# Moving the convolution tables, the joins and the query norms in the second block's input projections

## The reference, cut to what matters

```python
h  = modulate(x, norm1_g[l], sh1, sc1)           # 512 tokens
hc = modulate(ctx, norm1_g[l], csh1, csc1)       # 256 context tokens
zl_hy, zl_gla, zl_gdn = split_last(h @ w_in, IN_SIZES)
...
# Hyena: short_conv over z, then twice, with gate x1 and then x2:
conv = irfft(rfft(y, n=2*l) * filt_f[:, o], n=2*l)[:, :l]
y = gate * (conv + d_skip[o] * y)
# gated delta rule: q and k of each head are divided by their norms
shared = (l2norm(to_heads(q)) * GDN_D ** -0.5, l2norm(to_heads(k)), to_heads(v))
...
x = x + g1 * y
x = x + g2 * sq_relu_mlp(modulate(x, norm2_g[l], sh2, sc2), w_mlp1[l], w_mlp2[l])
```

## Time and profile before

| | |
|---|---|
| median of three runs | 1901.78 us (1901.45 to 1909.95) |
| the profiled execution | 1891.71 us |
| its span, first to last instruction | 1889.9 us |
| PE busy, share of the span | 1772.2 us, 94% |
| DVE, ACT, POOL busy | 52%, 34%, 19% |
| mean granted PE clock | 0.974 |
| projections of the second block | to about 1196 us |
| `stage_hyena` | 1196.6 to about 1235 us |

### The profile page before, as it was taken

How to read it: one execution, slowest core, us unless ns; L and a number is a source line. 1 busy time by engine, 2 the same in 40 slices (tenths; PEclk the granted TensorE clock), 3 DMA queues, 4 the chain that set the end, 5 groups by cost and what they waited for, 6 DMA issues and landing times. The chain is left out here.

```text
span 1889.9 us, 45257 instructions
## 1 busy us (share of the span) xinstructions
PE 1772.2 (94%) x19313; PEld 1322.5 (70%) x19313; DVE 989.0 (52%) x1839; ACT 651.8 (34%) x1233; POOL 361.6 (19%) x517
## 2 busy tenths in 40 slices
PE   6999989999989979989989998889998999999998
PEld 5777667777766763343357776677777788888887
DVE  7666445555467651121177876546777674323334
ACT  5555444534423222131245623022212343213421
POOL 1000053534444331101100000013222011001100
PEclk9999989999999989989999999889999999999999
DMA  6222111101139579999971223310001423222221
GB/s 230 81 92 77 58 52 48 43 22 52 53 130 360 199 299 374 410 407 409 408 295 56 84 79 106 122 36 14 25 21 53 169 100 123 96 94 94 96 100 45
DMA packets 77216, 265.11 MB, mean 140 GB/s; under 512 B 11552, under 2 KB 13984, under 8 KB 75744
## 3 DMA queue, kind: packets, MB, share of 16 engines
q1 hardware_dynamic: 65824, 233.92, 33.6%
q10 hardware_dynamic: 5616, 15.99, 2.4%
q0 software_dynamic: 5584, 12.40, 1.8%
HBM read 248.17 MB, written 21.50 MB: 143 GB/s over the span
## 5 line engine op out<-in xcount | busy, mean ns | idle before, releaser
L224 DVE TENSOR_TENSOR weights_lo<-ring,weights_hi 128x1024 fp32r<-128x1024 f32 (+1 forms) x134 | 165.8, 1240 | 139.5 <-ACT weights_hi L220 139.5
L220 ACT CAST weights_hi<-ring 128x1024 fp32r<-128x1024 f32 (+1 forms) x134 | 137.1, 1026 | 234.3 <-PE ps L250 223.0
L249 PE MATMUL ps<-wide_b_round,weights_hi 128*128 128x512 f32 (+1 forms) x368 | 134.6, 366 | 0.0
L248 PE MATMUL ps<-mlp_hi,weights_hi 128*128 128x512 f32 (+1 forms) x327 | 121.3, 371 | 1.2 <-DVE weights_lo L224 1.1
L249 PE MATMUL ps<-mlp_lo,weights_hi 128*128 128x512 f32 (+1 forms) x327 | 120.4, 368 | 0.0
L250 PE MATMUL ps<-mlp_hi,weights_lo 128*128 128x512 f32 (+1 forms) x327 | 120.4, 368 | 0.0
L248 PE MATMUL ps<-h_tail_round,weights_hi 128*128 128x512 f32 x232 | 90.8, 391 | 0.9 <-DVE weights_lo L224 0.7
L248 PE MATMUL ps<-wide_a_round,weights_hi 128*128 128x512 f32 x216 | 91.0, 422 | 0.6 <-DVE wide_b_round L742 0.6
L4706 POOL TENSOR_TENSOR h_scaled<-h_scaled 128x512 f32<-128x512 f32 x32 | 33.8, 1055 | 296.7 <-ACT h_scaled L4680 296.7
L249 PE MATMUL ps<-h_tail_rest_round,weights_hi 128*128 128x512 f32 x232 | 90.3, 389 | 0.0
L250 PE MATMUL ps<-h_tail_round,weights_lo 128*128 128x512 f32 x232 | 90.3, 389 | 0.0
(11 more groups left out here) (714 smaller groups left out, 4175.0 us busy)
## 6 DMA issues: line engine op xcount, KB each, us to landing
ring<-stream_in SPq DMA_DIRECT2D x207, 512.0 KB, 3.6
moe_ring<-stream_in SPq DMA_DIRECT2D x112, 512.0 KB
wide_b<-stream_in SPq DMA_DIRECT2D x32, 512.0 KB
w_mod<-w_mod_in ACTq DMA_DIRECT2D x24, 512.0 KB, 6.9
hy_mod<-w_mod_in SPq DMA_DIRECT2D x8, 512.0 KB, 6.9
gates_parked<-gates_late SPq DMA_DIRECT2D x14, 256.0 KB, 2.6
na_rel<-rel_in POOLq DMA_DIRECT2D x4, 640.0 KB, 4.1
xT<-xT_in SPq DMA_DIRECT2D x4, 512.0 KB, 5.9
```

Of the source, the lines that this page charges most:

```text
L220: act.copy(self.hi[:, i % self.n, at:], w[:, at:]).then_inc(self.cast.sem, self.cast.up())
L224: ins = eng.tensor_tensor(self.lo[:, i % self.n, at:], self.unit(i)[0][:, at:], self.hi[:, i % self.n, at:], ALU.subtract)
L248: pe.matmul(out, left[0], right[0], start=start, stop=False, **kw)
L249: pe.matmul(out, left[0], right[1], start=False, stop=False, **kw)
```

## The change

- SP: the filter and `hy_fwd` are issued ahead of the small moves, and all four quarters of `hy_inv` behind them, still ahead of the moves and all in the projections. They go to the three modulation slots and to a free row of `d_gate`, so they wait for the last modulation step and for the last sum of the query norms (`summed` 8).
- The sixteen modulation steps are over by unit 19; before, two of them lay in units 20 and 21.
- All four joins are on POOL.
- The query norms of the four heads, before after (20,1), (21,0), (21,1) and behind spectrum 1, are now after (21,0), (21,1), spectrum 1 and spectrum 2. DVE's order at the end is spectra 0, head 2, spectra 1, head 3.
- `stage_hyena` has no loads of `hy_inv`, and eight slots for its eight pieces of `w_mod`, so that SP waits for none of them.

```diff
-SIDE.update({at: ("qb", i) for i, at in enumerate(((20, 1), (21, 0), (21, 1), (22, 0)))})
+SIDE.update({at: ("qb", i) for i, at in enumerate(((21, 0), (21, 1), (22, 0), (22, 1)))})
...
-MOD_AT = {12: 2, 13: 1, 14: 1, 15: 2, 16: 2, 17: 1, 18: 2, 19: 3, 20: 1, 21: 1}
+MOD_AT = {12: 2, 13: 1, 14: 1, 15: 2, 16: 3, 17: 2, 18: 3, 19: 2}
...
-        inv = mod_slot[1:3]
+        inv = [mod_slot[1], mod_slot[2], mod_slot[0], d_gate[:, 1, :]]
... tensor
                 conv.spectrum(pe, 0)
                 conv.spectrum(pe, 1)
+                side(number["qb", 2])
+                conv.spectrum(pe, 2)
                 side(number["qb", 3])
-                conv.spectrum(pe, 2)
                 conv.spectrum(pe, 3)
... vector
-                    if u == N - 2:
-                        join(0)
-                        join(1)
                 leave(N - 1)
                 conv.spectra(dve, 0, 0)
+                side(number["qb", 2])
+                conv.spectra(dve, 0, 1)
                 side(number["qb", 3])
-                conv.spectra(dve, 0, 1)
... gpsimd
-                join(2)
-                join(3)
+                for i in range(4):
+                    join(i)
... sync
-                for f in range(LongConv.EARLY):
-                    sp.wait_ge(mod_stepped.sem, mod_stepped.at(MOD_STEPS - 2 + f))
-                    sp.dma_start(inv[f], k.dram["hy_inv"][:, f, :]).then_inc(inv_in.sem, inv_in.up(16))
                 sp.wait_ge(saved.sem, saved.at(16))
                 sp.wait_ge(w.done.sem, w.done.at(place["gk", 0] + 1))
                 sp.dma_start(k.B[:, :, :], k.dram["filter"]).then_inc(filter_in.sem, filter_in.up(16))
+                sp.wait_ge(k.used, k.after(N - 1))
+                for f in range(2):
+                    sp.dma_start(k.ring[:, 4 + f, :], k.dram["hy_fwd"][:, f, :]).then_inc(filter_in.sem, filter_in.up(16))
+                sp.wait_ge(mod_stepped.sem, mod_stepped.at(MOD_STEPS))
+                sp.wait_ge(summed.sem, summed.at(8))
+                for f in range(NF):
+                    sp.dma_start(inv[f], k.dram["hy_inv"][:, f, :]).then_inc(slot_in[(f + 1) % 3].sem, slot_in[(f + 1) % 3].up(16))
                 sp.wait_ge(pads.sem, pads.at(2))
                 sp.wait_ge(left_a.sem, left_a.at(place["gk", 0] + 1))
                 sp.wait_ge(left_v.sem, left_v.at(dve_before[place["gk", 0] + 1]))
                 ... the twelve small moves
-                sp.wait_ge(k.used, k.after(N - 1))
-                for f in range(2):
-                    sp.dma_start(k.ring[:, 4 + f, :], k.dram["hy_fwd"][:, f, :]).then_inc(filter_in.sem, filter_in.up(16))
... stage_hyena
-    SLOTS_W = 6
+    SLOTS_W = 8
...
-                for f in range(conv.EARLY, NF):
-                    sp.dma_start(late_inv[:, f - conv.EARLY, :], k.dram["hy_inv"][:, f, :]).then_inc(inv_in.sem, inv_in.up(16))
                 for n in range(DB):
-                    if n >= SLOTS_W:
-                        sp.wait_ge(mod_used.sem, mod_used.at(n - SLOTS_W + 1))
                     sp.dma_start(wm[:, n % SLOTS_W, :], k.dram["w_mod"][4 * DB + n]).then_inc(...)
...
-                    if o == 0 and f >= conv.EARLY:
-                        pe.wait_ge(inv_in.sem, inv_in.at(16 * (NF - conv.EARLY)))
```

More of the change, by code:

```diff
@@ L3107, in stage_mixer_in @@
             e_done, x_done, gate_chain = k.sig("e_done"), k.sig("gate_min_done"), k.sig("gate_chain")
-            mod_in, mod_stepped = [k.sig(f"mod_landed{i}") for i in range(3)], k.sig("mod_steps")
-            folds, inv_in = k.sig("hy_halves"), k.sig("inv_landed")
+            slot_in, mod_stepped = [k.sig(f"mod_landed{i}") for i in range(3)], k.sig("mod_steps")
+            folds = k.sig("hy_halves")
             def has_dve(i):
@@ L3444, in scale_x @@
                         h_scaled.sem, h_scaled.up())
[L3446 to L3449, removed]
                 def mod_step(m):
@@ L3453, in mod_step @@
                     c, x, total = k.silu_c[:, n, 0:1], mod_slot[m % 3], mod_total[:, half * T:(half + 1) * T]
-                    dve.wait_ge(mod_in[m % 3].sem, mod_in[m % 3].at(16 * (m // 3 + 1)))
+                    dve.wait_ge(slot_in[m % 3].sem, slot_in[m % 3].at(16 * (m // 3 + 1)))
                     if n == 0:
@@ L3539, in load_mod @@
                         sp.wait_ge(mod_stepped.sem, mod_stepped.at(m - 2))
-                    sp.dma_start(mod_slot[m % 3], k.dram["w_mod"][3 * DB + n][:, half * T:(half + 1) * T]).then_inc(mod_in[m % 3].sem, mod_in[m % 3].up(16))
+                    sp.dma_start(mod_slot[m % 3], k.dram["w_mod"][3 * DB + n][:, half * T:(half + 1) * T]).then_inc(slot_in[m % 3].sem, slot_in[m % 3].up(16))
                 a, n = MAT["gla_a2"]
@@ L3567, in _ @@
                     sp.dma_start(dst, src).then_inc(moved.sem, moved.up(16))
-                sp.wait_ge(k.used, k.after(N - 1))
-                for f in range(2):
-                    sp.dma_start(k.ring[:, 4 + f, :], k.dram["hy_fwd"][:, f, :]).then_inc(filter_in.sem, filter_in.up(16))
                 sp.wait_ge(filter_in.sem, filter_in.at(48))
-                sp.wait_ge(inv_in.sem, inv_in.at(32))
+                for landed in slot_in:
+                    sp.wait_ge(landed.sem, landed.last)
                 sp.wait_ge(moved.sem, moved.at(16 * 12))
@@ L3576, in stage_mixer_in, with stage_hyena @@
     return conv, inv, mod_total
-def stage_hyena(k, conv, early_inv, total, u, yT):
-    SLOTS_W = 6
+def stage_hyena(k, conv, inv, total, u, yT):
+    SLOTS_W = 8
     with ExitStack() as st:
-        late_inv = k.sb("hy_inv_late", [P, NF - conv.EARLY, T], st)
-        inv = [x.rearrange("p (i t) -> p i t", i=2) for x in (*early_inv, *(late_inv[:, f, :] for f in range(NF - conv.EARLY)))]
+        inv = [x.rearrange("p (i t) -> p i t", i=2) for x in inv]
         pq, by = k.sb("hy_pq", [P, 2, 2, HALF], st), k.sb("hy_by", [P, 2, 2, 2, HALF], st)
@@ L3589, in stage_hyena @@
         with k.block() as block:
-            inv_in, mod_in = k.sig("inv_landed"), [k.sig(f"mod_landed{i}") for i in range(SLOTS_W // 2)]
+            mod_in = [k.sig(f"mod_landed{i}") for i in range(SLOTS_W // 2)]
             v_ready, v_done = k.sig("v_ready"), k.sig("v_copied")
@@ L3597, in _ @@
             def _(sp):
-                for f in range(conv.EARLY, NF):
-                    sp.dma_start(late_inv[:, f - conv.EARLY, :], k.dram["hy_inv"][:, f, :]).then_inc(inv_in.sem, inv_in.up(16))
                 for n in range(DB):
-                    if n >= SLOTS_W:
-                        sp.wait_ge(mod_used.sem, mod_used.at(n - SLOTS_W + 1))
-                    sp.dma_start(wm[:, n % SLOTS_W, :], k.dram["w_mod"][4 * DB + n]).then_inc(mod_in[n // 2 % 3].sem, mod_in[n // 2 % 3].up(16))
+                    sp.dma_start(wm[:, n % SLOTS_W, :], k.dram["w_mod"][4 * DB + n]).then_inc(mod_in[n // 2].sem, mod_in[n // 2].up(16))
             @block.tensor
@@ L3635, in mods @@
                 def mods(n):
-                    pe.wait_ge(mod_in[n // 2 % 3].sem, mod_in[n // 2 % 3].at(32 * (n // SLOTS_W + 1)))
+                    pe.wait_ge(mod_in[n // 2].sem, mod_in[n // 2].at(32))
                     for m in range(DB):
```

## The result

| | before | after | ratio, 95% interval |
|---|---|---|---|
| first comparison, medians | 1905.17 us (4 runs) | 1878.42 us (4 runs) | 0.9895 (0.9864 to 0.9927) |
| second comparison | 1894.44 us (17 runs) | 1880.58 us (6 runs) | 0.9924 (0.9895 to 0.9953) |
| third comparison | 1897.94 us (11 runs) | 1880.83 us (6 runs) | 0.9912 (0.9890 to 0.9934) |
| profiled execution | 1891.71 us | 1887.80 us | |

The changed kernel is faster: by the ratios 0.8 to 1.0%, which is 20, 14 and 17 us in the order of the table. In the first comparison the two medians lie further apart than its ratio says (26.8 us, or 0.986); in the other two they agree with it (13.9 and 17.1 us). The forecast was 1884.4 us, 17.4 under a median of 1901.78; the median measured beside it is 1878.42.

What follows compares the result with a forecast made beforehand. PE, busy 94%, was taken to bound the kernel through waits and slow clock. 15.1 us at the projections' end plus 2.35 in `stage_hyena` made 17.4, giving 1884.4 us (own range 1881 to 1888, whole range 1877 to 1893).

Steps and rivals of the forecast that it cites:

- The end of the projections: Units 20 and 21 through the spectra: without PE's waits and slow clock, PE ends the stage 15.1 us sooner, at 1181.2.
- The tables: Filter and `hy_fwd` at the first spectrum: landed before PE asks at 1171.5, no wait; bounds 1.6 or 6.7 us.
- The moves: SP's twelve small moves at the projections' end: landed at 1180.5 to 1183.6, costed at nothing, 2.4 us kept for range.
- The joins: Four on POOL, 2.35 us each, ending at 1170.4: DVE not slowed, cost nothing; bound 2.4 us.
- The modulation steps: Moved to units 16 to 19, into DVE's idle time: price nothing; 0.74 us a step without cover.
- `stage_hyena`: Ways back at the stage's start: without the `hy_inv` load they take 7.9 us, a gain of 2.35 us.
- first three: Moves end the stage (1886.8 us, chance 0.10); tables still late (1892.9, 0.08); joins hold DVE (1886.8, 0.03).
- the last: Rival at the projections' end: slow joins make POOL end the stage, slower overall; chance 0.02.
- the formula: With joins of j us each, POOL ends the projections at 1161 + 4j, deciding over PE from j = 5.05 us.
- the fourth: Rival in later stages: the clock takes it back, 20 us more at 0.50 leaving 8 us gain, 1893.5 us; chance 0.05.
- a sign of being wrong: Listed: DMA wait at L3054 or the stage's end, POOL last at the stage's end, or `stage_recur` of another length.

Runs made afterwards that it cites:

- inv_late: Changed kernel with only quarters 2 and 3 of `hy_inv` loaded at the start of `stage_hyena` again; stretch from last rest to `stage_recur` 61.85 us, against 57.85.
- steps_late: Changed kernel with only the modulation steps back in units 16 to 21; stretch 61.43 us against 57.85, timed once at 1877.92 us.
- norms_early: Changed kernel with only the query norms put back half a unit, head 0 between units 20 and 21; stretch 61.83 and 61.58 us, against 57.85.
- moves_first: Changed kernel with `hy_fwd` issued behind the twelve small moves again; ratio 0.9971 to the kernel before, stretch 69.62 us against 57.85.

## Why the prediction was right

*The end of the projections* (forecast 15.1 us). By the table the stage starts at 21.44 in place of 36.95: 15.5 us. PE's path came out as written: last matmul at 21.1 behind the rest's start, where the forecast has 1181.2 - 1159.67 = 21.5. The reciprocal was in time (it ends at 1175.15 in the profile after, the first spreading starts at 1175.92), and head 0's product was done 2 us before head 1's spreading.

*The tables* (no wait taken, up to 6.7 us as a bound). None; they had some 3 us to spare, as forecast. `hy_fwd` took 6.6 us for the 6.5 taken, the filter 7.7 for 10.2. In the three executions of before, where the moves follow right behind it, the filter takes 10.2 to 10.6 us; in the eleven others, where they come later, 7.6 to 8.2.

*The moves* (cost nothing, up to 2.4 us as a bound). Nothing, with 4.5 us of cover. The landing shrank from a median of 6.8 us to 4.1, and issuing all twelve took 7.6 us where 8.9 was taken.

*The joins* (nothing). Right, by the reason given: no DVE instruction with two SBUF inputs runs beside them. This cover is thin. The first such instruction is that of the first spectra, 4.1 us after POOL is done, and the later modulation steps would have been others.

*The modulation steps* (nothing). The changed kernel loses nothing by them. That their move itself is worth 3.6 us of the stretch, because step 15 would hold SP's queue, I had not priced.

*`stage_hyena`* (2.35 us). The ways back are 2.25 us shorter, and so is the stage by 2.2. The slow stretch there stayed, at 1204 in place of 1212.

*The rivals.* None of the first three happened, nor the last. POOL as the end of the stage was tried with three times the work and behaves as the formula says. Of the fourth, that later stages take something back, there is a trace: `stage_recur` is longer, which the prediction names as a sign of being wrong. No run shows that this is clock.

*The total.* The 17.4 us were summed on one execution, and the three ratios say 14, 17 and 20. The median of 1878.42 lies in the whole range (1877 to 1893) and 2.6 us under the forecast's own, 1881 to 1888. Two things that the sum didn't have partly cancel. The mean stretch of before over three executions is 76.97 us, so that the change gains 19.1 there: the profiled execution of before happened to be the shortest of the three. And the tail, whose code is not changed, is 655.0 us on average before (three executions) and 658.0 after (three): 3.0 us lost. 19.1 - 3.0 is 16.1 us. So the closeness of 17.4 to the whole gain is in part luck; in the stretch it is not.

The loss is in `stage_recur`, 250.9 to 252.7 us before and 254.0 to 255.3 after; the stage behind it takes 403.3 to 403.5 in all 14 executions. Part of it is seen 178 to 200 us after the start of `stage_recur`: PE stands still in L922 with nothing that the profile shows to wait for, while six units stream into the ring. Before and after, in the view of waits:

```profile
PE ps L922 <- issue: 0.5, 1, 0.5
```

```profile
PE ps L922 <- issue: 2.7, 2, 1.3
```

It is 0.5, 1.1 and 1.1 us in the three executions of before and 2.7, 2.8 and 2.6 in those of after. Of the eight other executions, seven have 1.7 to 2.5, and inv_late, which gives PE's program in `stage_hyena` a wait for the late quarters back, has 0.8. That is 1.8 of the 3.0 us at most. And steps_late has 2.2 us of it and still the shortest `stage_recur` of all, 250.1 us. So neither the cause of these stops nor the rest of the loss is known, and three executions on each side do not show that the change is what lengthens `stage_recur`.

## What to carry to other kernels

A queue that is strictly in order should be read from the transfer that somebody waits for backwards: here the slot of `hy_fwd` was free 17 us before its transfer was issued, and two things stood ahead of it, a load that waits for a late DVE step, and twelve small moves that nobody waits for yet. With the moves ahead of it again the stretch was 11.8 us longer; with the late steps back, which then held only what stands behind `hy_fwd`, it was 3.6 us longer. A wait of PE costs itself for certain and the slow clock behind it sometimes, so price it with a range, from several executions. And compare profiles between two marks around the change, since the times of two executions of one kernel lie up to 14 us apart (1874.01 and 1887.80), nearly as much as the change is worth.

## What the runs showed of the hardware

- *Where the scatter lies.* In the 14 profiled executions the first matmul of L1109, early in `stage_core` (the recurrence of the first block), starts between 233.3 and 235.9 us, the first of L1230, further on in it, between 305.6 and 311.3, and the first of L1804, in the stage behind it, between 572.5 and 583.3, in code that is the same in all. From there to the last rest the distance differs by 3.2 us at most; that rest starts between 1158.7 and 1169.4. So most of the scatter of 11 us ahead of the change arises in that one stage. Why is not shown.
- *The slow clock moves about.* In one and the same kernel (norms_early) a 2.03 us wait was followed by a clock of 1.00 (2.4 GHz) or of 0.50 (1.2 GHz) for at least 6 us, and the execution that escaped it had more slow time later, in `stage_hyena`.
- *DVE beside POOL.* A DVE instruction of 0.42 us with two SBUF inputs took 2.38 beside a POOL instruction of 2.39, one of 0.74 took 2.69; with one SBUF input and PSUM (0.68 and 1.51 us) nothing changed, nor for a reciprocal in SBUF, which takes 3.34 us beside the joins and also at 1087.1, where POOL is idle.
- *Small moves.* The same twelve transfers land in 5.6 to 8.7 us with the filter just ahead, in 3.0 to 5.1 us when the large transfers are ahead of them and nearly through, and in 1.9 to 2.7 in moves_first, where the last large transfer left 6.8 us ahead of them. There `hy_fwd` is issued right behind them as it is before, so that alone does not make them slow.
